# The lambda sums of an attention layer, from TensorE to VectorE

## The chip, the cores and the metric

The kernel runs on one core of a Trainium2 chip. The metric is the device time of one execution in microseconds (us), from launch to end. A core has TensorE (PE) for matrix products, with its weight loads shown as PEld, VectorE (DVE), ScalarE (ACT), GpSimd (POOL) and SyncE (SP), which here only issues transfers. The engines run their own lists of instructions and wait for each other through semaphores; 16 DMA engines move data between the chip's main memory (HBM) and the on-chip memory (SBUF).

## The reference

Two layers on x of 256 rows by 2048, both x + Mixer(RMSNorm(x)): a gated differential attention with 8 heads, then a gated Conformer convolution, and a last RMSNorm. Only the attention is touched, and in it the scalar lambda:

```python
h = xn @ w_in
q, k, v, gate = jnp.split(h, ...)
lam = (jnp.exp(jnp.sum(lq1 * lk1))
       - jnp.exp(jnp.sum(lq2 * lk2)) + lambda_init)
...
s = einsum(q, k) + bias
p = softmax(s)
a = p[:, :, 0] - lam * p[:, :, 1]
o = einsum(a, v)
```

lq1, lk1, lq2 and lk2 are vectors of 128 numbers. So lambda needs two products of 128 numbers, two sums and two exponentials, once for the layer.

## The kernel before, in words

Every product of the layers is made in three passes: activations and weights are both split in a high and a low part, and PE multiplies high by high, high by low and low by high. The weights come in chunks of 1 MB (four blocks of 128 rows, 512 columns, `w_raw`), into a ring of four. SP loads a chunk when the low part of the chunk four before it is done; ScalarE makes the high part (`high_part`, L473), VectorE the low part (`low_part`, L814), and then PE multiplies.

The attention's first product is worked through in four pairs of heads. A pair has 16 slots, one chunk each: slots 0 to 3 make q, 4 to 7 k, 8 to 11 v, 12 to 15 the gate. `pair_slot(j, i)` exists on PE, ScalarE and VectorE and puts the attention's own work between the chunks: the scaling of k at slots 7 and 8, the scores (PE: L1327 to L1329; VectorE: L898, L901, L902) and the softmax's exponentials (ScalarE: L548) at slots 9 and 10, lambda and the weighting of the two softmaxes at slot 11 (L907 to L917), the transposes (L932) and a's split (L573, L936) at slots 12 and 13, and A·V on PE at slot 14 (L1341 to L1343). Chunk numbers run on: slot i of pair 0 multiplies chunk i, while ScalarE and VectorE split chunk i + 4 there. Pair 0 is unrolled, and its first four chunks come in 16 small pieces (`HEAD`).

For lambda the four vectors are four columns behind the other per-feature vectors in one transfer (`vec_all`, L351). VectorE multiplies them pairwise behind head piece 8 (L852, 128x2). PE multiplies a 128x128 matrix of ones by these two columns behind slot 2 (`lambda_sums`, L1216), which sums over the partitions and leaves the sums on all of them. ScalarE takes the Exp from that bank (L510), behind the split of chunk 5 and ahead of the squares of x (L519). VectorE puts them together at slot 11 (L907).

What sets the order near it is written out by hand. SP's list in pair 0 is: chunk loads, the two halves of x behind chunks 5 and 6, the taps of the convolution (`dwT`, L370) behind chunk 7, and the bias windows (`bias_w`, L376) behind chunk 13. The windows are first made in HBM: GpSimd writes a line per head (L437), ScalarE stores the lines (L512) and expands them (`windows_dram`, L558), and SP waits for that (`windows_stored`) before it loads the bias. VectorE's first score step (L898) waits for the bias.

The bank for the lambda sums is also the one in which the norm's factor is spread over the partitions behind slot 6 (`spread_rstd`, L1204); the counts `a_full` and `a_free` give it to one and then the other.

## Time and profile before

| | |
|---|---|
| median of 3 runs | 826.24 us (825.64 to 827.05) |
| the profiled execution's own time | 825.33 us |
| its span, first to last instruction | 823.5 us |
| PE busy | 815.9 us (99%) |
| VectorE busy | 645.0 us (78%) |
| ScalarE busy | 449.3 us (55%) |
| GpSimd busy | 228.8 us (28%) |
| mean granted clock of PE | 0.998 |
| HBM traffic | 200 GB/s over the span |

A row of the timeline has the start, the duration and the engine, then the line of the kernel, the operation, output<-inputs, the shapes and the count; in brackets stands how long the engine sat idle before it and what ended that. A busy share is a mean over stages with different limits, so the stretch around the change has to be read by itself. Matmuls overlap in the pipeline: the distance from one start to the next is what one costs. All times in the rows are from the span's start.

### The profile page before, as it was taken

How to read it: one execution, taken by the hardware profiler on the slowest of the kernel's cores; microseconds unless marked ns; L12 is line 12 of the kernel's file. 1: busy time of each engine (PE TensorE's matmuls, PEld its weight loads, DVE VectorE, ACT ScalarE, POOL GpSimd, SP SyncE). 2: the span in 40 equal slices, each digit the busy share in tenths (PEclk: the TensorE clock that was granted, in tenths of full speed). 3: DMA queues.
4: the chain of work that ended last, by engine and by line, in shares of the span. 5: the costliest groups of instructions: out<-in, count | busy, mean ns of one | idle time of the engine just before them, and what ended most of it. 6: DMA issues, size and time to landing. Idle time of an engine off the chain costs nothing.

```text
span 823.5 us, 13844 instructions
## 1 busy us (share of the span) xinstructions
PE 815.9 (99%) x5628; PEld 754.6 (92%) x5628; DVE 645.0 (78%) x1095; ACT 449.3 (55%) x586; POOL 228.8 (28%) x107
## 2 busy tenths in 40 slices
PE   9999999999999999999999999999999999999996
PEld 9988899889998899888888999999999999998885
DVE  7579785797659785798788988999999998656651
ACT  7756643546436643555554465465555556594432
POOL 0300000000000000002000009988989987680000
PEclk9999999999999999999999999999999999999999
DMA  9987566536754566535655666655655565549502
GB/s 330 395 304 260 175 210 217 184 122 204 232 187 145 171 209 217 186 103 175 229 174 190 205 194 216 204 175 186 205 190 175 200 197 176 192 155 355 197 8 102
DMA packets 99809, 163.68 MB, mean 199 GB/s; under 512 B 3616, under 2 KB 40992, under 8 KB 99240
## 3 DMA queue, kind: packets, MB, share of 16 engines
q1 hardware_dynamic: 98128, 160.51, 58.0%
q10 hardware_dynamic: 1624, 2.38, 0.8%
q8 instruction: 39, 0.64, 0.3%
q14 instruction: 18, 0.15, 0.1%
HBM read 160.76 MB, written 3.69 MB: 200 GB/s over the span
## 4 chain that ended last, share of the span: by engine, by line
PE 94%; DMA 2%; DVE 1%; ACT 1%; SPq 1%; issue 0%; ACTq 0%
PE ps_acc L1242 16%; PE ps_acc L1244 16%; PE ps_acc L1245 16%; PE ps_acc L1228 14%; PE ps_acc L1230 14%; PE ps_acc L1231 14%; DMA sb_xs<-in_x 2%; DMA sb_w_raw<-in_attn_w_in 1%; PE ps_a L1204 0%; PE ps_d L1327 0%; PE ps_d L1329 0%; PE ps_a L1341 0%; PE ps_a L1343 0%; PE ps_d L1328 0%; PE ps_a L1342 0%
## 5 line engine op out<-in xcount | busy, mean ns | idle before, releaser
L473 ACT ACTIVATE sb_w_hi<-sb_w_raw 128x2048 fp32r<-128x2048 f32 x139 | 265.7, 1919 | 224.0 <-PE ps_acc L1245 151.3
L445 POOL TENSOR_TENSOR sb_w_lo<-sb_w_raw,sb_w_hi 128x2048 fp32r<-128x2048 f32 x45 | 208.2, 4634 | 387.3 <-ACT sb_w_hi L473 387.3
L814 DVE TENSOR_TENSOR sb_w_lo<-sb_w_raw,sb_w_hi 128x2048 fp32r<-128x2048 f32 x94 | 213.6, 2289 | 91.7 <-ACT sb_w_hi L473 91.3
L1242 PE MATMUL ps_acc<-sb_conv_hi,sb_w_hi 128*128 128x256 f32 x768 | 213.0, 277 | 0.0
L1245 PE MATMUL ps_acc<-sb_conv_hi,sb_w_lo 128*128 128x256 f32 x768 | 212.1, 276 | 0.0
L1244 PE MATMUL ps_acc<-sb_conv_lo,sb_w_hi 128*128 128x256 f32 x768 | 212.1, 276 | 0.0
L1045 DVE SCALAR_TENSOR_TENSOR ps_d<-sb_uT,sb_dwT,ps_d 128x256 f32<-128x256 f32 x480 | 189.3, 517 | 4.5 <-ACT ps_d L704 4.5
L1228 PE MATMUL ps_acc<-sb_w_hi,sb_act_hi 128*128 128x512 f32 x384 | 149.7, 390 | 0.0
L1230 PE MATMUL ps_acc<-sb_w_lo,sb_act_hi 128*128 128x512 f32 x384 | 149.6, 390 | 0.0
L1231 PE MATMUL ps_acc<-sb_w_hi,sb_act_lo 128*128 128x512 f32 x384 | 149.4, 389 | 0.0
L1244 PEld LDWEIGHTS ps_acc<-sb_conv_lo,sb_w_hi 128*128 128x128 f32 x768 | 144.2, 188 | 0.0
L1242 PEld LDWEIGHTS ps_acc<-sb_conv_hi,sb_w_hi 128*128 128x128 f32 x768 | 144.2, 188 | 0.0
L1245 PEld LDWEIGHTS ps_acc<-sb_conv_hi,sb_w_lo 128*128 128x128 f32 x768 | 144.2, 188 | 0.0
L1242 PE MATMUL ps_acc<-sb_act_hi,sb_w_hi 128*128 128x256 f32 x448 | 123.8, 276 | 0.2 <-DVE sb_w_lo L814 0.2
L1245 PE MATMUL ps_acc<-sb_act_hi,sb_w_lo 128*128 128x256 f32 x448 | 123.7, 276 | 0.0
L1244 PE MATMUL ps_acc<-sb_act_lo,sb_w_hi 128*128 128x256 f32 x448 | 123.7, 276 | 0.0
L1231 PEld LDWEIGHTS ps_acc<-sb_w_hi,sb_act_lo 128*128 128x128 f32 x384 | 72.1, 188 | 15.1
L1228 PEld LDWEIGHTS ps_acc<-sb_w_hi,sb_act_hi 128*128 128x128 f32 x384 | 72.1, 188 | 14.9 <-DVE sb_act_lo L983 0.4
L1230 PEld LDWEIGHTS ps_acc<-sb_w_lo,sb_act_hi 128*128 128x128 f32 x384 | 72.1, 188 | 14.4
L1242 PEld LDWEIGHTS ps_acc<-sb_act_hi,sb_w_hi 128*128 128x128 f32 x448 | 84.1, 188 | 0.6 <-DVE sb_w_lo L814 0.5
L1244 PEld LDWEIGHTS ps_acc<-sb_act_lo,sb_w_hi 128*128 128x128 f32 x448 | 84.1, 188 | 0.1
L1245 PEld LDWEIGHTS ps_acc<-sb_act_hi,sb_w_lo 128*128 128x128 f32 x448 | 84.1, 188 | 0.0
(166 smaller groups left out, 875.3 us busy)
## 6 DMA issues: line engine op xcount, KB each, us to landing
sb_w_raw<-in_attn_w_in SPq DMA_DIRECT2D x59, 1024.0 KB, 5.8
sb_w_raw<-in_conv_w_in SPq DMA_DIRECT2D x64, 512.0 KB, 4.6
sb_w_raw<-in_attn_w_out SPq DMA_DIRECT2D x16, 1024.0 KB, 5.0
sb_w_raw<-in_conv_w_in SPq DMA_DIRECT2D x16, 1024.0 KB, 5.1
sb_w_raw<-in_conv_w_out SPq DMA_DIRECT2D x16, 1024.0 KB, 5.0
sb_w_raw<-in_attn_w_in SPq DMA_DIRECT2D x15, 256.0 KB, 4.6
sb_xs<-in_x SPq DMA_DIRECT2D x2, 1024.0 KB, 13.4
sb_x_in<-in_x_turned SPq DMA_DIRECT2D x15, 128.0 KB, 4.3
```

The lines of the kernel that those rows point to most:

```text
L445: pool.tensor_tensor(w_part(w_lo, c), w_raw[c % RING][:], w_part(w_hi, c).bitcast(F32), ALU.subtract).then_inc(lo_ready_pool, 1)
L473: act.activation(w_part(w_hi, c if like is None else like), w_raw[slot][:], ACT.Copy).then_inc(hi_ready, 1)
L814: dve.tensor_tensor(w_part(w_lo, like), w_raw[slot][:], w_part(w_hi, like).bitcast(F32), ALU.subtract).then_inc(lo_ready, 1)
L1045: dve.scalar_tensor_tensor(out_, uT[:, k, tap:tap + SEQ], dwT[:, k, tap:tap + 1], out_, ALU.mult, ALU.add).then_inc(tap_done, 1)
L1228: pe.matmul(into, left_hi, high[:, k], start=(kt == 0 and not filled), stop=False, skip_group_check=filled)
L1230: pe.matmul(into, left_hi, low[:, k], start=False, stop=False, skip_group_check=filled)
L1231: ins = pe.matmul(into, left_lo, high[:, k], start=False, stop=(kt == KT - 1), skip_group_check=filled)
L1242: pe.matmul(into, left_hi, hi[:, kt], start=(kt == 0 and f % 2 == 0), stop=False, skip_group_check=True)
L1244: pe.matmul(into, left_hi, lo[:, kt], start=False, stop=False, skip_group_check=True)
L1245: ins = pe.matmul(into, left_lo, hi[:, kt], start=False, stop=(kt == KT - 1), skip_group_check=True)
```

## The change

The four lambda vectors are an input of their own, laid end to end (512 numbers). SP reads them with one transfer whose source repeats for each of the 128 partitions, behind the load of chunk 8, into a part of `mT` that is not yet in use. At slot 9 of pair 0, ahead of the first score step, VectorE multiplies them pairwise along the free axis (128x256) and sums each half (128x2). ScalarE takes the Exp behind the softmax's exponentials of slot 10. The product with ones on PE, its wait and its bank hand-over go, as does the small product on VectorE. Semaphores are renamed and recounted with it.

```diff
-VECS_AT, LAM_AT = 4, 8
+VECS_AT = 4
...
-        lam_in = vec_all[:, 8 * KT:8 * KT + 4]
...
-        lam_prod = small[:, 4:6]
+        lam_sum = small[:, 4:6]
         lam_exp = small[:, 6:8]
         neg_lam = small[:, 8:9]
...
                 rstd_bc = mT[:, KT - 1]
+                lam_in = mT[:, KT - 3:KT - 1].rearrange("p a (b n) -> p (a b) n", b=2)
+                lam_prod = mT[:, KT - 4].rearrange("p (a n) -> p a n", a=2)
...
-        lam_prod_ready, lam_exp_ready = sem("lam_prod_ready"), sem("lam_exp_ready")
+        lam_landed, lam_prod_ready, lam_sum_ready = sem("lam_landed"), sem("lam_prod_ready"), sem("lam_sum_ready")
+        lam_exp_ready, neg_lam_ready, head_scaled = sem("lam_exp_ready"), sem("neg_lam_ready"), sem("head_scaled")
...
-        A_START, A_PER_PAIR = 2, 2
+        A_START, A_PER_PAIR = 1, 2
...
                 if p == VECS_AT:
-                    sp.dma_start(vec_all[:, 0:8 * KT + 4], vectors).then_inc(vecs_landed, 16)
+                    sp.dma_start(vec_all[:, 0:8 * KT], vectors).then_inc(vecs_landed, 16)
             sp.dma_start(table[:], rel_bias).then_inc(table_landed, 16)
...
                         if first and t == 1 and i == NCH - 1:
                             sp.dma_start(dwT[:], taps).then_inc(taps_landed, 16)
+                        if first and t == 2 and i == 0:
+                            sp.dma_start(lam_in, bass.AP(lambdas.tensor, lambdas.offset, [[0, P], [1, 4 * HD]])
+                                         ).then_inc(lam_landed, 16)
                         if (t, i) == ((3, 1) if first else (0, NCH - 1)):
                             if first:
                                 sp.wait_ge(windows_stored, 16)
...
-            act.wait_ge(a_full, 1)
-            act.activation(lam_exp, bank_a[0][:, 0:2], ACT.Exp).then_inc(a_free, 1)
             act.wait_ge(line_ready, len(bucket_runs()) + 1)
             act.dma_start(line_dram, line[:]).then_inc(line_stored, 16)
 
             act.activation(vecs[:, G_HEAD, :], vecs[:, G_HEAD, :], ACT.Copy, scale=1.0 - LAMBDA_INIT
-                           ).then_inc(lam_exp_ready, 1)
+                           ).then_inc(head_scaled, 1)
...
                                            ).then_inc(exp_done, 1)
+                    if type(j) is int and (j, i) == (0, 10):
+                        act.wait_ge(lam_sum_ready, 1)
+                        act.activation(lam_exp, lam_sum, ACT.Exp).then_inc(lam_exp_ready, 1)
                     return
...
                 if i == 7:
-                    act.wait_ge(a_full, 2)
+                    act.wait_ge(a_full, 1)
                     act.activation(rstd_bc, bank_a[0][:, 0:SEQ], ACT.Copy).then_inc(a_free, 1)
-                    act.wait_ge(a_free, 2 + 2)
+                    act.wait_ge(a_free, 2 + 1)
                 pair_slot(0, i)
...
-                if p == LAM_AT:
-                    dve.wait_ge(vecs_landed, 16)
-                    dve.tensor_tensor(lam_prod, lam_in[:, 0:4:2], lam_in[:, 1:4:2], ALU.mult
-                                      ).then_inc(lam_prod_ready, 1)
...
                     if type(j) is int and j == 0:
-                        dve.wait_ge(a_free, 2 + 2)
+                        dve.wait_ge(a_free, 2 + 1)
                     dve.wait_ge(w_free, RING + NCH * (4 * j + 2))
...
+                if i == 9 and type(j) is int and j == 0:
+                    dve.wait_ge(lam_landed, 16)
+                    dve.tensor_tensor(lam_prod, lam_in[:, 0:4:2], lam_in[:, 1:4:2], ALU.mult).then_inc(lam_prod_ready, 1)
+                    dve.wait_ge(lam_prod_ready, 1)
+                    dve.tensor_reduce(lam_sum, lam_prod, AX.X, ALU.add).then_inc(lam_sum_ready, 1)
                 if i == 8:
...
                 if i == 11:
                     if type(j) is int and j == 0:
-                        dve.wait_ge(a_free, 2 + 1)
+                        dve.wait_ge(lam_exp_ready, 1)
                         dve.scalar_tensor_tensor(neg_lam, lam_exp[:, 1:2], -LAMBDA_INIT, lam_exp[:, 0:1],
-                                                 ALU.add, ALU.subtract).then_inc(lam_prod_ready, 1)
-                        dve.wait_ge(lam_prod_ready, 2)
+                                                 ALU.add, ALU.subtract).then_inc(neg_lam_ready, 1)
+                        dve.wait_ge(neg_lam_ready, 1)
 
                     dve.wait_ge(exp_done, 8 * (j + 1))
                     link(dve.reciprocal(row_inv, row_sum))
...
-            def free_a(n):
-                pe.wait_ge(a_free, n + 1)
...
-            def lambda_sums():
-
-                free_a(0)
-                pe.wait_ge(lam_prod_ready, 1)
-                pe.matmul(bank_a[0][:, 0:2], ones[:], lam_prod, start=True, stop=True).then_inc(a_full, 1)
...
             for i in range(16):
                 pair_slot(0, i)
-                if i == 2:
-                    lambda_sums()
                 if i == 6:
-                    spread_rstd(1, 1)
+                    spread_rstd(0, 1)
...
-                               ("attn_head_gain", "conv_dw_b", "conv_ln_g", "conv_ln_b", "conv_b_in",
-                                "attn_lq1", "attn_lk1", "attn_lq2", "attn_lk2")])
+                               ("attn_head_gain", "conv_dw_b", "conv_ln_g", "conv_ln_b", "conv_b_in")])
+    lambdas = np.concatenate([inputs[name].reshape(-1) for name in ("attn_lq1", "attn_lk1", "attn_lq2", "attn_lk2")])
...
         "vectors": features.T,
+        "lambdas": lambdas,
```

VectorE, around slot 9 of pair 0, before: w_lo0 is the low part of chunk 12, ps_d0 and ps_d1 are the banks of the scores.

```order
L814 TENSOR_TENSOR sb_w_lo0<-sb_w_raw0,sb_w_hi0 128x2048 [waits hi_ready]
L898 SCALAR_TENSOR_TENSOR sb_probs<-ps_d0,sb_small,sb_bias_w 128x512 [waits d_full,a_full,bias_landed]
L901 TENSOR_REDUCE sb_small<-sb_probs 128x2 [waits d_free]
L902 TENSOR_SCALAR sb_small<-sb_small 128x2 [waits dve_done]
L898 SCALAR_TENSOR_TENSOR sb_probs<-ps_d1,sb_small,sb_bias_w 128x512 [waits d_full]
L901 TENSOR_REDUCE sb_small<-sb_probs 128x2 [waits d_free]
```

And with the change, from the same low part on:

```order
L820 TENSOR_TENSOR sb_w_lo0<-sb_w_raw0,sb_w_hi0 128x2048 [waits hi_ready]
L887 TENSOR_TENSOR sb_mT<-sb_mT 128x256 [waits lam_landed]
L889 TENSOR_REDUCE sb_small<-sb_mT 128x2 [waits lam_prod_ready]
L905 SCALAR_TENSOR_TENSOR sb_probs<-ps_d0,sb_small,sb_bias_w 128x512 [waits d_full,a_full,bias_landed]
L908 TENSOR_REDUCE sb_small<-sb_probs 128x2 [waits d_free]
L909 TENSOR_SCALAR sb_small<-sb_small 128x2 [waits dve_done]
L905 SCALAR_TENSOR_TENSOR sb_probs<-ps_d1,sb_small,sb_bias_w 128x512 [waits d_full]
L908 TENSOR_REDUCE sb_small<-sb_probs 128x2 [waits d_free]
```

Two operations stand between chunk 12's low part and the first score step; `mT` holds the vectors and the products. The first has a wait for the new transfer.

SP in pair 0, from chunk 5's load on, before (in_x is x by rows, in_taps the taps, window_scratch the bias windows):

```order
L342 DMA sb_w_raw<-in_attn_w_in 128x4x512 [waits lo_ready]
L368 DMA sb_xs<-in_x 128x2048
L342 DMA sb_w_raw<-in_attn_w_in 128x4x512 [waits lo_ready]
L368 DMA sb_xs<-in_x 128x2048
L342 DMA sb_w_raw<-in_attn_w_in 128x4x512 [waits lo_ready]
L370 DMA sb_dwT<-in_taps 128x496
L342 DMA sb_w_raw<-in_attn_w_in 128x4x512 [waits lo_ready] x6
L376 DMA sb_bias_w<-window_scratch 128x2x384 [waits windows_stored]
```

And with the change:

```order
L344 DMA sb_w_raw<-in_attn_w_in 128x4x512 [waits lo_ready]
L370 DMA sb_xs<-in_x 128x2048
L344 DMA sb_w_raw<-in_attn_w_in 128x4x512 [waits lo_ready]
L370 DMA sb_xs<-in_x 128x2048
L344 DMA sb_w_raw<-in_attn_w_in 128x4x512 [waits lo_ready]
L372 DMA sb_dwT<-in_taps 128x496
L344 DMA sb_w_raw<-in_attn_w_in 128x4x512 [waits lo_ready]
L374 DMA sb_mT<-in_lambdas 128x512
L344 DMA sb_w_raw<-in_attn_w_in 128x4x512 [waits lo_ready] x5
L381 DMA sb_bias_w<-window_scratch 128x2x384 [waits windows_stored]
```

One transfer has come between chunk 8's load and the five that follow it, ahead of the bias; it waits for nothing of its own.

ScalarE between chunk 5's split and chunk 6's, before (ps_a is the bank of the lambda sums):

```order
L473 ACTIVATE sb_w_hi<-sb_w_raw 128x2048 [waits w_free,chunk_landed1]
L510 ACTIVATE sb_small<-ps_a 128x2 [waits a_full]
L512 DMA line_scratch<-sb_line 8x512 [waits line_ready]
L514 ACTIVATE sb_vec_all<-sb_vec_all 128x16
L519 ACTIVATE sb_probs,sb_small<-sb_xs 128x2048 [waits rows_landed0]
L473 ACTIVATE sb_w_hi<-sb_w_raw 128x2048 [waits w_free,chunk_landed2,ss_ready]
```

And with the change:

```order
L478 ACTIVATE sb_w_hi<-sb_w_raw 128x2048 [waits w_free,chunk_landed1]
L515 DMA line_scratch<-sb_line 8x512 [waits line_ready]
L517 ACTIVATE sb_vec_all<-sb_vec_all 128x16
L522 ACTIVATE sb_probs,sb_small<-sb_xs 128x2048 [waits rows_landed0]
L478 ACTIVATE sb_w_hi<-sb_w_raw 128x2048 [waits w_free,chunk_landed2,ss_ready]
```

The Exp at the second row and its wait for PE are gone; it now stands behind the last Exp of slot 10.

## Rows read from the trace of the kernel before

**Rows 1.** The page's part 1: busy time, share of the span, instructions

```profile
PE 815.9 (99%) x5628; PEld 754.6 (92%) x5628; DVE 645.0 (78%) x1095; ACT 449.3 (55%) x586; POOL 228.8 (28%) x107
```

**Rows 2.** Waits of PE: waiter <- releaser: us in total, times, longest

```profile
PE ps_d L1348 <- POOL sb_ones L423: 1.0, 1, 1.0
PE ps_acc L1242 <- DVE sb_w_lo L814: 0.2, 1, 0.2
```

**Rows 3.** Timeline of PE, 21 to 91 us: start, duration, instruction

```profile
21.37 0.28 PE L1216 MATMUL ps_a<-sb_small,sb_ones 128*128 128x2 f32 x2
21.51 0.70 PE L1291 MATMUL ps_acc<-sb_act_hi,sb_w_hi 128*128 128x256 f32 x4
...
43.99 0.39 PE L1242 MATMUL ps_acc<-sb_act_hi,sb_w_hi 128*128 128x256 f32 x1 [0.25 <-DVE sb_w_lo L814]
...
90.46 0.28 PE L1341 MATMUL ps_a<-sb_v_hi,sb_q_hi 128*128 128x256 f32 x1
```

**Rows 4.** The chain that ended last, 17 to 45 us: start, us

```profile
19.39 15.62 DMA sb_xs<-in_x
...
41.64 2.30 DVE sb_w_lo L814
```

**Rows 5.** Timeline of VectorE, 14 to 90 us

```profile
14.65 0.15 DVE L852 TENSOR_TENSOR sb_small<-sb_vec_all 128x2 f32<-128x2 f32 x1
...
59.30 2.29 DVE L814 TENSOR_TENSOR sb_w_lo<-sb_w_raw,sb_w_hi 128x2048 fp32r<-128x2048 f32 x1 [1.04 <-ACT sb_w_hi L473]
62.49 0.75 DVE L898 SCALAR_TENSOR_TENSOR sb_probs<-ps_d,sb_small,sb_bias_w 128x512 f32<-128x512 f32 x1 [0.90 <-DMA sb_bias_w<-window_scratch]
63.28 0.69 DVE L901 TENSOR_REDUCE sb_small<-sb_probs 128x2 f32<-128x512 f32 x1
...
68.20 0.75 DVE L898 SCALAR_TENSOR_TENSOR sb_probs<-ps_d,sb_small,sb_bias_w 128x512 f32<-128x512 f32 x1 [0.26 <-PE ps_d L1329]
...
71.36 2.28 DVE L814 TENSOR_TENSOR sb_w_lo<-sb_w_raw,sb_w_hi 128x2048 fp32r<-128x2048 f32 x1
...
75.43 0.48 DVE L917 SCALAR_TENSOR_TENSOR sb_probs<-sb_probs,sb_small 128x256 f32<-128x256 f32 x1
75.83 0.35 DVE L915 TENSOR_SCALAR sb_probs<-sb_probs,sb_small 128x256 f32<-128x256 f32 x1
...
88.79 1.29 DVE L936 TENSOR_TENSOR sb_q_lo<-sb_probs,sb_q_hi 128x512 fp32r<-128x512 f32 x2 [0.70 <-ACT sb_q_hi L573]
```

**Rows 6.** Timeline of ScalarE, 28 to 76 us

```profile
28.84 0.14 ACT L510 ACTIVATE sb_small<-ps_a 128x2 f32<-128x2 f32 x1
...
35.03 1.93 ACT L519 ACTIVATE sb_probs<-sb_xs 128x2048 f32<-128x2048 f32 x1 [0.56 <-DMA sb_xs<-in_x]
...
74.34 1.27 ACT L568 ACTIVATE sb_v_hi<-ps_acc,sb_small 128x512 fp32r<-128x512 f32 x2 [1.76 <-PE ps_acc L1231]
```

**Rows 7.** Timeline of SP's queue, 23 to 60 us: start of issue, us

```profile
23.42 3.16 SPq L370 DMA_DIRECT2D sb_dwT<-in_taps  x1
26.65 0.40 SPq L342 DMA_DIRECT2D sb_w_raw<-in_attn_w_in  x1
...
31.29 1.26 SPq L342 DMA_DIRECT2D sb_w_raw<-in_attn_w_in  x1
...
59.55 0.37 SPq L376 DMA_DIRECT2D sb_bias_w<-window_scratch  x1
```

**Rows 8.** DMA issues: count, KB each, median us from issue to landing

```profile
sb_w_raw<-in_attn_w_in SPq DMA_DIRECT2D x59, 1024.0 KB, 5.8
...
sb_b_out_bc<-in_conv_b_out SPq DMA_DIRECT2D x1, 1024.0 KB, 7.1
...
sb_vec_all<-in_vectors SPq DMA_DIRECT2D x1, 66.0 KB, 4.3
```

**Rows 9.** Windows: length, busy PE, PEld, DVE, ACT, POOL, PEclk, DMA share, GB/s

```profile
46.00:54.00 8.00, 8.00 (x53) 7.24 (x52) 5.78 (x5) 3.39 (x3) 0.00 (x0) 1.00 1.03 372
54.00:64.00 10.00, 10.00 (x52) 8.50 (x51) 7.23 (x7) 6.90 (x6) 0.00 (x0) 1.00 0.61 209
```

More of the change, by code:

```diff
@@ L72, in bucket_runs, with build @@
     return [(at, upto, int(bucket[at])) for at, upto in zip(starts, starts[1:] + [rel.size])]
-def build(nc, x, x_turned, vectors, taps, final_gain, rel_bias, attn_w_in, attn_w_out, conv_w_in,
+def build(nc, x, x_turned, vectors, lambdas, taps, final_gain, rel_bias, attn_w_in, attn_w_out, conv_w_in,
           conv_w_out, conv_b_out, out):
```

## The prediction

> **What bounds the kernel now.** I read the totals first, then TensorE's waits, then its rows in order of time, then the engines that hand it work in pair 0, and last the DMAs. TensorE (PE) is busy for 815.9 of 823.5 us [rows 1]. Its whole list of waits has two lines, 1.0 us before the first matmul and 0.2 us once for a low part of the weights [rows 2]; the second is the 0.25 us ahead of the matmul at 43.99 us [rows 3]. So an edit moves the end in only three ways: it takes matmuls off the stream, it changes one of these two waits, or it makes a new one. The rest of the 7.6 us that PE isn't busy lies after its last matmul, where nothing is edited.
>
> The wait at 43.99 is the start of chunk 7. The chain that ended last runs through it: the transfer of the second half of x ends at 35.01, ScalarE squares it at 35.03, then come the root, the q copies and chunk 7's split on ScalarE, and VectorE's low part at 41.64, done at 43.94 [rows 4, 6]. What releases PE there is a transfer in the full DMA queue, and no lambda step.
>
> **The matmul that goes.** The matmul of 128x2 starts at 21.37 and the next one starts at 21.51 [rows 3]: 0.14 us of PE. It pays nothing as long as the next stop stands: PE comes to chunk 7 at 43.6 instead of 43.74 and waits 0.39 us instead of 0.25. Value taken: 0. If the cover were gone (chunk 7 ready in time) it would be a gain of 0.14, with the wait 0.39. That is the lower bound of the whole change.
>
> **What goes from the other engines.** VectorE loses a product of 128x2 (0.15 us at 14.65, [rows 5]) and ScalarE an Exp (0.14 us at 28.84, [rows 6]). Both lie ahead of 35.03, where ScalarE idles for the x transfer anyway (0.56 us, [rows 6]); 0. The Exp moves behind the eight of pair 0's second score slot, which use the same function, so I count no table load, and 0.14 us there. ScalarE then stands idle for 1.76 us until the next v copy [rows 6], which covers it. The vectors' transfer of 66 KB [rows 8] loses 2 KB, 3% of it; 0.
>
> **The transfer that is added.** 128 rows of 2 KB, 256 KB, go on SP's queue between chunk 8's load (issued 26.65) and chunk 9's (31.29) [rows 7]. SP has 4.2 us there, since chunk 9's load waits for a low part. The slowest issue in sight, that of the taps, took 3.16 us [rows 7], so even that would not delay chunk 9's issue. The data do delay what follows: the DMA share is 1.03 from 46 to 54 us at 372 GB/s [rows 9]. At that rate 262144 B are 0.70 us of all engines. Nearest row for the price: weights have the same rows of 2 KB and make up this stretch. Other end: the one broadcast in the trace (b_out, also 128 rows, 8 KB each) took 7.1 us to land [rows 8], 1.8 us for a quarter of the bytes, or all 7.1 if rows and not bytes set it. I take 0.70 and keep both ends; call it d.
>
> The Trainium skill's page "DMA: Bandwidth & Descriptors", section "Anatomy of one DMA — SWDGE (gpsimd) path", gives a transfer some 2.0 us of fixed cost beside its bytes at 436 GB/s; it speaks of transfers that GpSimd issues. By it the estimate for this one is 2.6 us; were all of that time taken from the queue, d would be 2.6. The 16 engines' share near 1.0 at 372 GB/s says that one transfer's fixed part lies beside the next one's data, so I don't add it; what it would do is part of the second rival.
>
> Which loads are late by d: chunks 9 to 13, the window store (ScalarE's queue, same DMA engines) and behind it the bias load, which SP issues at 59.55 when the store is done [rows 7]. From 54 to 64 us the share is only 0.61 [rows 9], so the store could also make up some of d. The weights have room: chunk 12's low part ends at 61.59 [rows 5], and PE takes chunk 12 only when chunk 11 is done, at 74.3 by the v copy that waits for it [rows 6].
>
> **The two VectorE operations that are added.** Product 128x256: between 0.35 (one tensor with a scalar, 128x256) and 0.48 (two tensors, 128x256) [rows 5], 0.42. Reduction of 128x256 to 128x2: one of 128x512 is 0.69 [rows 5], so between 0.35 and 0.69, 0.43 with a fixed part. Two hand-overs of 0.04: 0.93 us, bounds 0.75 to 1.25. They stand behind chunk 12's low part and ahead of the first score step. There VectorE idles 0.90 us, from 61.59 to 62.49, for the bias load [rows 5]. Without d the sum is then 61.59 + 0.93 + 0.04 = 62.56, 0.07 late. With d both sides move: chunk 12 lands 0.7 later, and so does the bias: the score step starts at about 63.26, 0.77 late.
>
> **What is late next.** Behind the score step on VectorE stand all of pair 0's softmax, the 16 transposes and a's low part, and PE waits for the last at its A·V step. On the way one idle gives some back: 0.26 us at 68.20, where VectorE waits for PE's scores, which are not later [rows 5]. Nothing else does: the 0.70 us at 88.79 waits for ScalarE, which waits for the transposes. a's low part ends at 90.08 (88.79 + 1.29, [rows 5]); PE starts A·V at 90.46 without a wait [rows 3]. With the 0.05 us of a hand-over (43.94 to 43.99, [rows 3, 4]) the room is 0.33. So the new wait is 0.77 - 0.26 - 0.33 = 0.18 us, and in general d - 0.52, if that is above 0. The next lambda step (the 128x1 operation ahead of the reciprocal) was there before. It now waits for the Exp, which comes 0.2 us after the last softmax Exp (done at 72.58, the 74.34 of the v copy less its 1.76 of idle time, [rows 6]), at some 72.8 before any delay; VectorE is busy with chunk 14's low part until 73.64 [rows 5], so 0.
>
> Behind pair 0 VectorE idles for more than a microsecond at a time, and the later pairs are as before. A wait of PE is never given back, since PE is busy to the end.
>
> **Sum.** Against the profiled execution of 825.33 us (span 823.5, 1.8 us around it): 0 for the matmul + 0.18 for the wait = 825.5. That execution lies 0.9 us under the median of the runs, 826.24; on the median the forecast is 826.4.
>
> **Rivals.**
> First, all hidden: the window store makes up d in its half-empty stretch, the bias lands at 62.5 as before, and only 0.07 us of lateness is left, less than the 0.26. For it: share 0.61 from 54 to 64 [rows 9]. Against: the store's own end is what SP waits for, so something paces it. Time 826.2.
>
> Second, slower: the broadcast holds the queues much longer than its bytes. Mechanism: all 128 rows read the same 2 KB, as b_out's read one row. Everything turns on A·V at 90.46: from d = 0.52 on PE waits d - 0.52, and from d = 2.2 on that is over 0.2%. With 1.8 us the wait is 1.3 and the time 827.5; with 7.1 it is 6.6 and 832.8. For it: 7.1 us to landing against 5.8 for as many bytes of weights [rows 8]. Against: b_out's landing holds time queued behind weights too. By the page named above (2.6 us) the wait would be 2.1 and the time 828.3; the trace so far speaks for a fixed part that lies beside other data.
>
> Third, faster: in the full queue of the head the x transfer ends earlier. The smaller vectors rows are the only thing in front of it, at most 66 KB at 372 GB/s, 0.18 us; with the matmul's 0.14 that is 0.32, and 0.39 if the wait goes wholly. Time 825.9. Against: just 2 KB leave, and any time that PE gains at 43.99 is lost in part at 90.46, since the bias does not come earlier.
>
> **How the numbers follow.** No change means within 0.2%, 1.65 us, about what a measurement of this kernel can tell. Forecast (a small wait at A·V, 0 to 0.5 us) 0.62; all hidden 0.20; slower 0.10, of which 0.08 is beyond 1.65 us; faster 0.08, of which 0.03 is left for more than the 0.39 that I can find. So 0.03 faster, 0.89 same, 0.08 slower. The runs of before lie from 0.6 under to 0.8 over their median. The range takes the third rival with that spread (825.9 - 0.6) and the second with its 1.8 us and some of it: 825.3 to 827.8.
>
> **What would show it.** Right: PE's row at the start of chunk 7 with a wait of about 0.4 us instead of 0.25, at the same time near 44.0; two new VectorE rows of 0.4 us each between chunk 12's low part and the first score step; the score step near 63.3; a wait of 0 to 0.5 us ahead of A·V at 90.5; the bias issue 0 to 0.7 us later than 59.55. Wrong: a wait at A·V over 1 us (d mis-sized), chunk 7 starting well ahead of 44 (the head's queue moved), or any new wait of PE behind pair 0.

## The result and the profile after

The changed kernel takes 827.49 us (median of 20 runs, 826.41 to 829.2), the kernel before 826.21 us (20 runs beside them, 825.32 to 829.07). The ratio is 1.0014 with an interval of 1.0008 to 1.0020: inside 0.2%, and yet measurably slower, by some 1.3 us. The forecast of 826.4 us was 1.1 us too low; the time lies inside the stated range of 825.3 to 827.8. The profiled execution took 827.74 us (span 826.0), against 825.33 us (span 823.5). These two executions lie 2.41 us apart and the medians 1.28, so the sizes read from the rows are those of one pair of executions.

The page's totals after, to be held against [rows 1]:

```profile
PE 816.1 (99%) x5626; PEld 754.5 (91%) x5626; DVE 645.6 (78%) x1096; ACT 449.1 (54%) x586; POOL 229.6 (28%) x107
```

PE's busy time is the same to 0.2 us, so the difference is waiting. Its whole list of waits (waiter, releaser: us in total, times, longest) has three lines where [rows 2] had two:

```profile
PE ps_a L1339 <- issue: 1.6, 1, 1.6
PE ps_d L1346 <- POOL sb_ones L428: 1.0, 1, 1.0
PE ps_acc L1240 <- DVE sb_w_lo L820: 0.9, 1, 0.9
```

The first is new, and it is pair 0's A·V step. The last is the start of chunk 7. The rows of both on PE's timeline (start, duration, instruction, idle time before it):

```profile
44.59 0.38 PE L1240 MATMUL ps_acc<-sb_act_hi,sb_w_hi 128*128 128x256 f32 x1 [0.87 <-DVE sb_w_lo L820]
...
92.81 0.36 PE L1339 MATMUL ps_a<-sb_v_hi,sb_q_hi 128*128 128x256 f32 x1 [1.58 <-issue]
```

A·V starts 2.35 us after the 90.46 of [rows 3]. Of that, 1.58 is the new wait and 0.77 PE brought along; 0.60 of the 0.77 is the later chunk 7. The list puts the wait down to "issue", so it names no releaser. VectorE's timeline shows what A·V waited for: a's low part, the last row here, is done at 92.70, 0.11 us before A·V starts (before: [rows 5]):

```profile
60.49 2.29 DVE L820 TENSOR_TENSOR sb_w_lo<-sb_w_raw,sb_w_hi 128x2048 fp32r<-128x2048 f32 x1 [0.97 <-ACT sb_w_hi L478]
...
62.70 0.42 DVE L887 TENSOR_TENSOR sb_mT<-sb_mT 128x256 f32<-128x256 f32 x1
63.15 0.42 DVE L889 TENSOR_REDUCE sb_small<-sb_mT 128x2 f32<-128x256 f32 x1
...
65.46 0.75 DVE L905 SCALAR_TENSOR_TENSOR sb_probs<-ps_d,sb_small,sb_bias_w 128x512 f32<-128x512 f32 x1 [1.89 <-DMA sb_bias_w<-window_scratch]
...
70.82 0.74 DVE L905 SCALAR_TENSOR_TENSOR sb_probs<-ps_d,sb_small,sb_bias_w 128x512 f32<-128x512 f32 x1
...
91.41 1.29 DVE L943 TENSOR_TENSOR sb_q_lo<-sb_probs,sb_q_hi 128x512 fp32r<-128x512 f32 x2 [0.70 <-ACT sb_q_hi L579]
```

The two added operations take 0.42 us each and hold up nothing: behind them VectorE still waits 1.89 us for the bias. The first score step comes 2.97 us later than before, at 65.46. The idle 0.26 us that [rows 5] show at 68.20 is gone from the second step (70.82), so it was given back; the rest, up to a's low part, runs as before to within 0.1 us. So the sum is 2.97 - 0.26 (given back) - 0.33 (room at A·V) - 0.77 (PE later itself) = 1.61, and the row says 1.58. The bias is late because it is issued late. SP's queue after (start of issue, time for which SP is held, transfer; before: [rows 7]):

```profile
23.75 3.70 SPq L372 DMA_DIRECT2D sb_dwT<-in_taps  x1
27.50 0.58 SPq L344 DMA_DIRECT2D sb_w_raw<-in_attn_w_in  x1
28.12 4.98 SPq L374 DMA_DIRECT2D sb_mT<-in_lambdas  x1
33.15 0.57 SPq L344 DMA_DIRECT2D sb_w_raw<-in_attn_w_in  x1
37.38 0.37 SPq L344 DMA_DIRECT2D sb_w_raw<-in_attn_w_in  x1
44.56 0.37 SPq L344 DMA_DIRECT2D sb_w_raw<-in_attn_w_in  x1
...
62.44 0.37 SPq L381 DMA_DIRECT2D sb_bias_w<-window_scratch  x1
```

The added transfer holds SP for 4.98 us, chunk 9's load goes out at 33.15 instead of 31.29, and the bias at 62.44 instead of 59.55. The rows at 37.38 and 44.56 are the loads of chunks 10 and 11. ScalarE's rows show where the window store is issued and the load that comes late most visibly, chunk 10's (L478), first after the change, then before it:

```profile
39.22 0.80 ACTq L564 DMA_DIRECT2D window_scratch<-line_scratch  x1
...
49.25 1.93 ACT L478 ACTIVATE sb_w_hi<-sb_w_raw 128x2048 fp32r<-128x2048 f32 x1 [2.34 <-DMA sb_w_raw<-in_attn_w_in]
```

```profile
38.63 0.80 ACTq L558 DMA_DIRECT2D window_scratch<-line_scratch  x1
...
46.33 1.93 ACT L473 ACTIVATE sb_w_hi<-sb_w_raw 128x2048 fp32r<-128x2048 f32 x1 [0.57 <-DMA sb_w_raw<-in_attn_w_in]
```

So the store lasts, from its issue to the bias issue that waits for it, 20.9 us before and 23.2 us after. It starts 0.6 us later and runs 2.3 us longer: that is the whole lateness of the bias. The question for the experiments is what makes the store longer.

### The profile page after: what moved, and what is told of

It is laid out like the page before. It is cut to its first block, busy times and chain, and to the rows that moved or that the text cites. A ratio compares the mean times of both kernels' runs of the same rounds, so it can differ in the third digit from the quotient of the medians.

```text
span 826.0 us, 13841 instructions
## 1 busy us (share of the span) xinstructions
PE 816.1 (99%) x5626; PEld 754.5 (91%) x5626; DVE 645.6 (78%) x1096; ACT 449.1 (54%) x586; POOL 229.6 (28%) x107
## 4 chain that ended last, share of the span: by engine, by line
PE 94%; DMA 2%; DVE 1%; ACT 1%; SPq 1%; issue 1%; ACTq 0%
PE ps_acc L1240 16%; PE ps_acc L1243 16%; PE ps_acc L1242 16%; PE ps_acc L1226 14%; PE ps_acc L1228 14%; PE ps_acc L1229 14%; DMA sb_xs<-in_x 2%; DMA sb_w_raw<-in_attn_w_in 1%; PE ps_a L1339 0%; PE ps_a L1211 0%; PE ps_d L1327 0%; PE ps_d L1325 0%; PE ps_a L1341 0%; PE ps_d L1326 0%; PE ps_a L1340 0%
## 5 line engine op out<-in xcount | busy, mean ns | idle before, releaser
L478 ACT ACTIVATE sb_w_hi<-sb_w_raw 128x2048 fp32r<-128x2048 f32 x139 | 265.5, 1918 | 224.5 <-PE ps_acc L1243 151.4
```

Source lines behind the costliest of these rows:

```text
L478: act.activation(w_part(w_hi, c if like is None else like), w_raw[slot][:], ACT.Copy).then_inc(hi_ready, 1)
```

## Experiments

The theories. **Bytes:** the 256 KB take DMA time from the store, more than the 0.70 us that I priced, because of when they come. **One row:** 128 reads of the same 2 KB are slow. **Held SP:** not the data but the 4.98 us for which SP can't issue chunk 9's load pushes the loads into the store. **Compute:** the moved operations, not the transfer. All eleven kernels were timed against the kernel before on the same chip. In each diff "-" is the changed kernel's code, unless it says otherwise. A table of all stands behind them.

**The changed kernel again.**

> The changed kernel once more. It separates what belongs to the change from what was chance in its one profile. If the late start of chunk 7 there (44.59 instead of 43.99 us) was chance of the head's transfers, chunk 7 starts at 43.9 to 44.2 here; if it belongs to the change, at 44.5 to 44.7. In both cases the wait of PE ahead of A.V should be there, 0.5 to 2 us, and the time 1.0 to 1.6 us over the kernel before.

827.48 us against 826.19, ratio 1.0014 (1.0004 to 1.0023). The profiled execution took 830.66 us. The list of waits:

```profile
PE ps_a L1339 <- issue: 2.1, 1, 2.1
...
PE ps_acc L1240 <- DVE sb_w_lo L820: 1.0, 1, 1.0
```

SP's queue:

```profile
30.28 3.40 SPq L374 DMA_DIRECT2D sb_mT<-in_lambdas  x1
...
63.64 0.37 SPq L381 DMA_DIRECT2D sb_bias_w<-window_scratch  x1
```

The same wait at the same place, and a store of 23.7 us (issued at 39.91).

**The kernel before again.**

> The kernel before once more, for a second profile of it. The profiles of the changed kernel and of the two experiments without or with the transfer alone have chunk 7 on PE at 44.6 to 45.4 us, the run with 128 different rows at 43.7. If that is chance of the head's transfers, this profile may also lie anywhere from 43.7 to 45.4; if it belongs to the change, it is again at 43.9 to 44.1. Either way no wait ahead of A.V, bias issue 20 to 22 us after the window store's issue, and a ratio of 1 within 0.1%.

826.48 against 826.49, 0.9996 (0.9987 to 1.0005). PE comes to A·V without a wait, as before:

```profile
90.96 0.28 PE L1341 MATMUL ps_a<-sb_v_hi,sb_q_hi 128*128 128x256 f32 x1
```

Chunk 7 starts at 44.46 here and at 43.99 in [rows 3]: the same kernel scatters by half a microsecond in the head. (The expectation above has 43.7 for the run with 128 different rows; its trace has 44.19.)

**Everything but the transfer.** GpSimd fills the room with a constant instead of lambda.

```diff
-                        if first and t == 2 and i == 0:
-                            sp.dma_start(lam_in, bass.AP(lambdas.tensor, lambdas.offset, [[0, P], [1, 4 * HD]])
-                                         ).then_inc(lam_landed, 16)
+            pool.wait_ge(lo_ready, RING + 1)
+            pool.memset(lam_in, 0.03).then_inc(lam_landed, 16)
```

> Leaves the transfer of the lambda vectors out: GpSimd fills their place with a constant in the time in which it has nothing to do, so lambda has another value. All the VectorE and ScalarE work of the change stays. Theory T (the added transfer makes the window store end late, and through the bias A.V): bias issue back at 59 to 60 us, no wait at A.V, 826.2 +- 0.4. Rival O (the two added VectorE operations take the room ahead of A.V): wait and time as in the changed kernel, 827.3 to 827.7. My recorded sum would give 826.2 here too.

826.69 against 826.19, 1.0004 (0.9995 to 1.0012): not told from no change. The store is back to 20.5 us. SP's queue:

```profile
59.97 0.37 SPq L378 DMA_DIRECT2D sb_bias_w<-window_scratch  x1
```

PE's row at A·V:

```profile
91.29 0.28 PE L1338 MATMUL ps_a<-sb_v_hi,sb_q_hi 128*128 128x256 f32 x1
```

No wait at A·V. It comes 0.83 us later than in [rows 3] because chunk 7 started at 44.82, without any added transfer.

**The transfer alone**, in the kernel before ("+" against that one); its data go unused, and VectorE only waits for them at the lambda step.

```diff
+                        if first and t == 2 and i == 0:
+                            sp.dma_start(lam_wide, bass.AP(lambdas.tensor, lambdas.offset, [[0, P], [1, 4 * HD]])
+                                         ).then_inc(lam_landed, 16)
...
+                        dve.wait_ge(lam_landed, 16)
```

> The kernel before, with only the new transfer at its place in SP's list, landing in the same unused memory; VectorE waits for it at slot 11, long after it is there. Theory T: bias issue 61.5 to 62.5 instead of 59.55, a wait at A.V of 0.5 to 2 us, 827.0 to 827.7. Rival O: no wait, 826.2 +- 0.3.

827.44 against 826.19, 1.0015 (1.0005 to 1.0024): the whole loss, with none of the moved operations. SP's queue:

```profile
28.16 5.80 SPq L374 DMA_DIRECT2D sb_mT<-in_lambdas  x1
...
62.39 0.37 SPq L381 DMA_DIRECT2D sb_bias_w<-window_scratch  x1
```

PE's row at A·V:

```profile
92.92 0.36 PE L1347 MATMUL ps_a<-sb_v_hi,sb_q_hi 128*128 128x256 f32 x1 [0.83 <-issue]
```

With the run without the transfer this rules out the compute theory. The wait at A·V is shorter (0.83), as PE itself is 1.63 us late there: chunk 7 started at 45.41.

**128 different rows** in place of one row read 128 times.

```diff
-                            sp.dma_start(lam_in, bass.AP(lambdas.tensor, lambdas.offset, [[0, P], [1, 4 * HD]])
-                                         ).then_inc(lam_landed, 16)
+                            sp.dma_start(lam_in, lambdas.rearrange("p (a n) -> p a n", n=HD)).then_inc(lam_landed, 16)
...
-        "lambdas": lambdas,
+        "lambdas": np.broadcast_to(lambdas, (P, 4 * HD)),
```

> The changed kernel, but its input holds the 512 numbers 128 times and the transfer reads 128 different rows of 2 KB. Rival R (128 reads of one row are slow): the issue no longer blocks SP for 5 us, the bias issue is back near 60, time 826.3 +- 0.4. Theory T: nothing changes, 827.2 to 827.8, SP blocked for 4 to 5 us.

827.11 against 826.19, 1.0011 (1.0001 to 1.0021). SP's queue:

```profile
27.35 5.08 SPq L374 DMA_DIRECT2D sb_mT<-in_lambdas  x1
...
61.81 0.37 SPq L380 DMA_DIRECT2D sb_bias_w<-window_scratch  x1
```

PE's row at A·V:

```profile
92.23 0.36 PE L1338 MATMUL ps_a<-sb_v_hi,sb_q_hi 128*128 128x256 f32 x1 [1.38 <-issue]
```

SP is held as long (5.08 us), the store lasts 23.3 us as in the changed kernel (23.2) and the wait is there. The one-row theory falls.

**The transfer on ScalarE's queue**, so that SP isn't held.

```diff
-                            sp.dma_start(lam_in, bass.AP(lambdas.tensor, lambdas.offset, [[0, P], [1, 4 * HD]])
-                                         ).then_inc(lam_landed, 16)
+            act.wait_ge(lo_ready, RING + 1)
+            act.dma_start(lam_in, bass.AP(lambdas.tensor, lambdas.offset, [[0, P], [1, 4 * HD]])).then_inc(lam_landed, 16)
```

> The changed kernel with the transfer issued from ScalarE's queue behind the store of the lines, at about 29 us, in place of SP's. Same bytes, same time, but SP is not held up. Theory I (SP is blocked for 5 us by the issue, so the loads of chunks 9 and 10 come later and fall into the time in which the window store would run fast): chunk 9 issued at 31 to 32 us, bias issue 20 to 21 us after the store's, no wait at A.V, 826.2 to 826.7. Rival B (the bytes alone do it): bias issue 22 to 24 us after the store's, wait of 0.8 to 2 us, 827.1 to 827.6.

827.22 against 826.49, 1.0007 (0.9998 to 1.0016). ScalarE's queue:

```profile
29.54 0.36 ACTq L514 DMA_DIRECT2D sb_mT<-in_lambdas  x1
```

SP's queue:

```profile
31.73 1.55 SPq L344 DMA_DIRECT2D sb_w_raw<-in_attn_w_in  x1
...
61.91 0.37 SPq L378 DMA_DIRECT2D sb_bias_w<-window_scratch  x1
```

PE's row at A·V:

```profile
92.26 0.36 PE L1338 MATMUL ps_a<-sb_v_hi,sb_q_hi 128*128 128x256 f32 x1 [1.06 <-issue]
```

The issue costs 0.36 us, chunk 9's load goes out near its old time (31.73), and still the store lasts 22.7 us and A·V waits 1.06. So the held SP is at most a part of it. How large a part stays open: the time lies between the two kernels, and its interval holds both.

**The transfer 21 us later**, behind chunk 13's load and ahead of SP's wait for the store.

```diff
-                        if first and t == 2 and i == 0:
-                            sp.dma_start(lam_in, bass.AP(lambdas.tensor, lambdas.offset, [[0, P], [1, 4 * HD]])
-                                         ).then_inc(lam_landed, 16)
...
                             if first:
+                                sp.dma_start(lam_in, bass.AP(lambdas.tensor, lambdas.offset, [[0, P], [1, 4 * HD]])
+                                             ).then_inc(lam_landed, 16)
                                 sp.wait_ge(windows_stored, 16)
```

> The changed kernel with the transfer issued by SP behind the load of chunk 13, just ahead of the wait for the window store, where the DMA engines are half idle. Theories I and B alike: bias issue 20 to 21.5 us after the store's; the vectors land at 58 to 61.5, so VectorE waits little for them; wait at A.V 0 to 0.5, 826.2 to 826.8. Rival O (added VectorE work): 827.3 or more.

826.12 against 826.49, 0.9997 (0.9987 to 1.0007). SP's queue:

```profile
49.38 0.68 SPq L375 DMA_DIRECT2D sb_mT<-in_lambdas  x1
...
59.19 0.37 SPq L380 DMA_DIRECT2D sb_bias_w<-window_scratch  x1
```

VectorE's first score step:

```profile
63.60 0.75 DVE L904 SCALAR_TENSOR_TENSOR sb_probs<-ps_d,sb_small,sb_bias_w 128x512 f32<-128x512 f32 x1 [0.43 <-DMA sb_bias_w<-window_scratch]
```

PE's row at A·V:

```profile
91.07 0.28 PE L1338 MATMUL ps_a<-sb_v_hi,sb_q_hi 128*128 128x256 f32 x1
```

The same bytes, beside the same store, cost nothing here: 19.95 us of store and no wait at A·V. The time of the kernel before is back; the interval lies clear of the changed kernel's 1.0008 to 1.0020, though it touches that of the second measurement, 1.0004 to 1.0023. It isn't the bytes as such, but when they come.

**The transfer behind the bias load, the product on GpSimd, the sums on ScalarE.**

```diff
+            pool.wait_ge(lam_landed, 16)
+            pool.tensor_tensor(lam_prod, lam_in[:, 0:4:2], lam_in[:, 1:4:2], ALU.mult).then_inc(lam_prod_ready, 1)
...
+                        for a in range(2):
+                            act.activation(lam_in[:, a], lam_prod[:, a], ACT.Copy, accum_out=lam_sum[:, a:a + 1]
+                                           ).then_inc(lam_sum_ready, 1)
...
-                    dve.tensor_tensor(lam_prod, lam_in[:, 0:4:2], lam_in[:, 1:4:2], ALU.mult).then_inc(lam_prod_ready, 1)
-                    dve.tensor_reduce(lam_sum, lam_prod, AX.X, ALU.add).then_inc(lam_sum_ready, 1)
```

> The transfer behind the bias load, GpSimd makes the product, ScalarE the sums (two copies of 128x128 with a running sum behind slot 9's exponentials, in idle time). Neither the window store nor VectorE's path to A.V has anything added. Theories I and B: no wait at A.V, 826.0 to 826.5, the kernel before within noise. If 827 or more, the loss has another source than the store and the path (the missing matmul, the order of ScalarE, the instructions' places).

826.16 against 826.49, 0.9998 (0.9989 to 1.0007). GpSimd's product:

```profile
67.10 2.54 POOL L454 TENSOR_TENSOR sb_mT<-sb_mT 128x256 f32<-128x256 f32 x1 [37.94 <-DMA sb_mT<-in_lambdas]
```

The split of chunk 14 on ScalarE, then its low part on VectorE:

```profile
70.97 1.92 ACT L480 ACTIVATE sb_w_hi<-sb_w_raw 128x2048 fp32r<-128x2048 f32 x1 [0.60 <-DMA sb_w_raw<-in_attn_w_in]
...
72.92 2.29 DVE L827 TENSOR_TENSOR sb_w_lo<-sb_w_raw,sb_w_hi 128x2048 fp32r<-128x2048 f32 x1 [0.71 <-ACT sb_w_hi L480]
```

PE's row at A·V:

```profile
91.75 0.36 PE L1341 MATMUL ps_a<-sb_v_hi,sb_q_hi 128*128 128x256 f32 x1 [0.77 <-issue]
```

Time as before, yet with a wait of 0.77 at A·V in its profile, where none was expected. VectorE waits 0.71 us for the split of chunk 14. ScalarE's added sums are done before that split, which waits 0.60 us for its load; and that load now stands behind the bias and the added transfer in SP's list. Taking work off VectorE gained nothing, as VectorE's 0.84 us were free.

**The transfer twice.**

```diff
+                            sp.dma_start(lam_spare, bass.AP(lambdas.tensor, lambdas.offset, [[0, P], [1, 4 * HD]])
+                                         ).then_inc(lam_landed, 16)
...
-                    dve.wait_ge(lam_landed, 16)
+                    dve.wait_ge(lam_landed, 32)
```

> The changed kernel with the transfer made twice, one behind the other, into two places (512 KB). Theory B (its bytes push the loads of chunks 9 and 10 into the time in which the window store would run fast): the store takes longer again, 24 to 26 us from its issue to the bias issue (20.5 to 20.9 before, 23.2 changed), wait at A.V 2.5 to 4 us, 828 to 830. Rival F (the store has lost its fast stretch already, more bytes cost only their own time, 0.7 us): 23.5 to 24.2 us, wait about 2.2, 827.8 to 828.5. If the store's end had nothing to do with the bytes: as the changed kernel, 827.5.

827.75 against 826.18, 1.0023 (1.0013 to 1.0033): 0.3 us over the changed kernel, which the intervals don't tell apart. PE's wait:

```profile
PE ps_a L1342 <- issue: 1.9, 1, 1.9
```

SP's queue:

```profile
27.21 5.10 SPq L375 DMA_DIRECT2D sb_mT<-in_lambdas  x1
32.35 0.57 SPq L377 DMA_DIRECT2D sb_mT<-in_lambdas  x1
...
61.85 0.37 SPq L384 DMA_DIRECT2D sb_bias_w<-window_scratch  x1
```

The second 256 KB add little: the store lasts 23.5 us, not 25 or more. It looks as if the first transfer had already taken something that can be lost only once.

**The store issued earlier**, behind chunk 6's split.

```diff
+                    act.wait_ge(line_stored, 16)
+                    act.dma_start(windows_dram, bass.AP(line_dram.tensor, line_dram.offset + P - 1,
+                                                       [[REL, HEADS], [-1, P], [1, BW]])).then_inc(windows_stored, 16)
...
-                if i == 4 and type(j) is int and j == 0:
-                    act.wait_ge(line_stored, 16)
-                    act.dma_start(windows_dram, bass.AP(line_dram.tensor, line_dram.offset + P - 1,
-                                                       [[REL, HEADS], [-1, P], [1, BW]])).then_inc(windows_stored, 16)
```

> The changed kernel with the transfer where it is, but ScalarE issues the window store behind the split of chunk 6, at 34 to 35 us instead of 39.2. If the chain store -> bias -> score step -> A.V is what costs, the bias is issued some 2 to 4 us earlier than 62.4 and the wait at A.V is gone or under 0.4 us: 826.0 to 826.7, although the transfer is still there. Rival: the earlier store only takes room from x and chunk 7, PE waits longer there (1 us or more at 43.6) and the time stays at 827 or above.

827.69 against 826.18, 1.0016 (1.0005 to 1.0027): no cure, where 826.0 to 826.7 was expected. The bias goes out at 56.61 and A·V has no wait, which supports the chain, but PE waits at the scores instead, for a k part that comes behind chunk 10's late split. PE's wait:

```profile
PE ps_d L1323 <- DVE sb_k_lo L892: 1.6, 1, 1.6
```

ScalarE's split of chunk 10:

```profile
51.87 1.92 ACT L478 ACTIVATE sb_w_hi<-sb_w_raw 128x2048 fp32r<-128x2048 f32 x1 [2.66 <-DMA sb_w_raw<-in_attn_w_in]
```

**The late transfer, the early store, and chunk 7's split ahead of the second square.**

```diff
+                                sp.dma_start(lam_in, bass.AP(lambdas.tensor, lambdas.offset, [[0, P], [1, 4 * HD]])
+                                             ).then_inc(lam_landed, 16)
                                 sp.wait_ge(windows_stored, 16)
...
+                    act.wait_ge(line_stored, 16)
+                    act.dma_start(windows_dram, bass.AP(line_dram.tensor, line_dram.offset + P - 1,
+                                                       [[REL, HEADS], [-1, P], [1, BW]])).then_inc(windows_stored, 16)
+                    high_part(RING + 3, 3, 2)
...
-            high_part(RING + 3, 3, 2)
...
-                if i == 6:
+                if i == 7:
                     spread_rstd(0, 1)
```

> A version that could beat both: the transfer behind chunk 13's load, the window store early, and chunk 7's split on ScalarE and VectorE ahead of the second square of x and the root, with the spread of the norm's factor behind slot 7 instead of 6. Then neither A.V nor chunk 7 (0 to 1 us of wait in the profiles so far) has anything to wait for, and the 0.14 us of the missing matmul count: 825.2 to 825.9, 0.04 to 0.12% under the kernel before. Rival: chunk 7's load itself lands too late for it, PE waits as before, 826.0 to 826.5; or the factor comes too late for k, a new wait at slots 8 to 10, 826.5 or more.

826.21 against 826.18, 1.0002 (0.9993 to 1.0010). PE's list has one line left, that before the first matmul:

```profile
PE ps_d L1343 <- POOL sb_ones L427: 1.0, 1, 1.0
```

The wait at chunk 7 is gone, and the time isn't the 825.2 to 825.9 that was expected: it is that of the kernel before. A gain of 0.25 us for the wait would be too little to tell here. No kernel here beats the one before.

**What the runs say together.** "Store" is the time from the store's issue to the bias issue.

| kernel | transfer issued at | store, us | A·V starts (wait) | median - before |
|---|---|---|---|---|
| before | none | 20.9 | 90.46 (0) | 0 |
| before again | none | 20.5 | 90.96 (0) | 0.0 |
| no transfer | none | 20.5 | 91.29 (0) | +0.5 |
| behind chunk 13 | 49.38 | 19.95 | 91.07 (0) | -0.4 |
| behind the bias | 61.04 | 21.7 | 91.75 (0.77) | -0.3 |
| changed | 28.12 | 23.2 | 92.81 (1.58) | +1.3 |
| changed again | 30.28 | 23.7 | 94.06 (2.13) | +1.3 |
| transfer alone | 28.16 | 22.3 | 92.92 (0.83) | +1.25 |
| 128 rows | 27.35 | 23.3 | 92.23 (1.38) | +0.9 |
| ScalarE's queue | 29.54 | 22.7 | 92.26 (1.06) | +0.7 |
| twice | 27.21, 32.35 | 23.5 | 92.23 (1.9) | +1.6 |
| store early | 27.35 | 23.4 | no wait; 1.58 at the scores | +1.5 |
| late transfer, early store | 51.59 | 23.5 | 90.36 (0) | 0.0 |

With the transfer at its early place the store takes 22.3 to 23.7 us, without it there 19.95 to 21.7 (the two kernels with an early store are left out; they come below). Where the 2.3 us arise in the changed kernel shows in the packets. Counted in the trace, in steps of 2 us of the span: packets of the window store (1024 of 1536 B in all) and the packets of 2048 B of SP's queue:

```
from, us          40   42   44   46   48   50   52   54   56   58   60
before   store     0   55  180  222  110  116  114  114   98   15    0
         SP      374  320  130  179  275  268  311  187  124  161
after    store     0   27  108  172  119  112  119  109  116  108   34
         SP      381  347  239  195  269  276  297  232  124  119
later    store     0   25  221  260  109  114  116  113   60    6
 (x 13)  SP      379  349   98  106  272  280  298  306  167  195
twice    store     0   65  111  121  117  109  117  114  116  112   42
         SP      280  314  291  307  309  277  259  266  112  114
```

("Later" is the transfer behind chunk 13.) Beside loads the store runs at 55 to 60 packets per us. In these kernels it runs faster only from 44 to 48 us, at up to 130, and SP's queue runs low there: chunk 11's load is issued only when chunk 7's low part is done, at 43.96 before and 44.56 after. Before, 402 packets went in these 4 us, after, 280. The missing 122, at 57 per us, are 2.1 us, about the 2.3 us by which the store is longer. The late loads (chunk 10's above all) now fill the gap. With the transfer twice the gap is gone, which fits that more bytes cost little more. Behind chunk 13 the transfer is issued when the gap has passed, and the gap is intact.

The gap isn't the whole account, as three runs show. Cut the store at its 800th packet. In the kernel before, the first 800 take 11.1 us and the last 224 take 5.05; in the changed kernel 13.1 and 5.3, so there the loss lies in the front part, with the gap. But with the transfer alone it is 11.2 and 6.25, and on ScalarE's queue 11.3 and 6.6: the front part is as before, and the store is late in its last packets, for a reason that these runs don't show (the last 224 also scatter without an early transfer, from 5.05 to 6.1). And with the late transfer and the early store, SP's queue falls just as low from 48 to 50 us (104 packets), and the store doesn't run faster: it moves 104 packets there. In both kernels with an early store it has no fast stretch at all and takes 23.4 and 23.5 us, with the transfer early or late. So it is shown that, with the store issued where it was, the transfer at its early place makes it longer; that it does so by closing the gap is read off the changed kernel's trace, and no run shows it by itself.

The rate itself isn't explained. The Trainium skill's page "DMA: Bandwidth & Descriptors", section "Queues, rings and completion order", says that each DMA engine takes turns between the queues that have work for it. The trace of the kernel before agrees with it in the gap (up to 130 packets per us against 57 beside loads), but that of the kernel with the late transfer and the early store from 48 to 50 us doesn't, and neither does the end of the store after the change: from 56 to 60 us, SP's queue has fallen from 297 to 124 packets in 2 us, and the store stays at 116 and 108. The windows (length, busy PE, PEld, DVE, ACT, POOL, granted clock, DMA share, GB/s) say the same:

```profile
56.00:58.00 2.00, 2.00 (x11) 1.65 (x10) 1.98 (x1) 1.03 (x2) 0.00 (x0) 1.00 0.56 216
58.00:60.00 2.00, 2.00 (x11) 1.65 (x10) 1.52 (x3) 1.46 (x1) 0.00 (x0) 1.00 0.53 204
```

The engines stand half idle in the stretch in which the store ends late. So something else than their share paces it there; what, stays open.

## Why the prediction was nearly right, and where it failed

- **The place and the chain were right.** The only new wait of PE is at A·V, by way of the store, the bias and the first score step. The formula held: with the lateness that the profile shows it gives 1.61, the row 1.58. The 0.26 given back and the 0.33 of room were as read.
- **The step that failed is "I take 0.70 and keep both ends; call it d".** I counted the transfer's bytes at the full queue's rate. The store alone became 2.3 us longer (2.8 in the second profile of the changed kernel), and the bias issue 2.89 us later instead of 0 to 0.7. The prediction's own sign of a mis-sized d, a wait at A·V over 1 us, came. The row that I had gives the bytes' share of a full queue, but the store doesn't end by that: before the change more than a third of it went in 4 us in which SP's queue runs low, and in the changed kernel much of that stretch was lost. An average over 46 to 54 us [rows 9] hides it. Why the transfer alone and the one on ScalarE's queue lose their time later, in the store's last packets, stays open. Of the values that I kept, 0.70 and 1.8 lie under the 2.3 and only 7.1 over it. That the time is still inside the range is luck: the range reaches up to it only by the 1.8 of the second rival, whose mechanism the runs don't bear out.
- **"So even that would not delay chunk 9's issue" failed too.** I priced the issue by the taps' 3.16 us [rows 7] as the slowest in sight; it took 4.98, and the next load was 1.86 us late. As the run on ScalarE's queue shows, this is at most a part of the cause.
- **The first rival was wrong.** The store made up nothing in its half-empty stretch: after the change the engines' share is 0.56 and 0.53 from 56 to 60 us, and the store keeps its 54 to 58 packets per us.
- **The second rival had about the right time (827.5) by the wrong mechanism.** It put the price on reading one row 128 times; 128 different rows cost the same. The estimate that the prediction worked out from the Trainium skill's page "DMA: Bandwidth & Descriptors" (section "Anatomy of one DMA — SWDGE (gpsimd) path"), 2.6 us, comes near the measured 2.3, but the runs don't bear out a fixed cost taken from the queue: then the place 21 us later would have cost it too (19.95 us of store), and two transfers twice of it (23.5).
- **The added VectorE work was right:** 0.42 and 0.42 us against 0.42 and 0.43. I had let it make the score step 0.07 late without d; with the late transfer, where the store isn't longer, VectorE still waits 0.43 us for the bias behind it.
- **The matmul was worth nothing, as said.** It is gone, and the wait at chunk 7 took it up. But I expected chunk 7 "at the same time near 44.0" and it came at 44.59. The runs put it from 43.72 (the transfer twice) to 45.41 (the transfer alone), 44.82 without any transfer; that is scatter of the head, and I had no row for it from one profile. What causes it is open.
- **The wait for the Exp** was priced at 0, and PE has no wait behind A·V.

## What to carry to other kernels

Before pricing an added transfer by its bytes, look at what else shares the DMA engines, in steps of 2 us and queue by queue: a transfer that something waits for may have a short fast stretch, and an added transfer ahead of it can cost more than its own bytes (here 2.3 us of store against 0.70 by bytes). The same transfer, issued behind the last load that the head is short of, was free here, so the first thing to try with a small transfer that isn't needed soon is another place for it in the issue order. Read the scatter of a head from more than one profile before calling half a microsecond there an effect.

## What the runs showed of the hardware

- A DRAM-to-DRAM store in packets of 1536 B ran at 55 to 60 packets per us (57 x 1536 B = 88 GB/s) beside a stream of loads and also when the loads thinned out. At up to 130 (200 GB/s) it ran only between 44 and 50 us, while SP's queue ran low; in another stretch as low, 48 to 50 us of the kernel with the late transfer and the early store, it ran at 52.
- In the two thin stretches in which the store didn't speed up, both queues moved about equally many packets: 224 of the store and 243 of SP's from 56 to 60 us after the change, 104 and 104 from 48 to 50 us in the kernel with the late transfer and the early store.
- Issuing a 256 KB transfer behind chunk 8's load held SP for 3.40 to 5.80 us, a second one right behind it for 0.57; later ones held SP for 0.68 (at 49.38), 0.51 (at 51.59) and 0.76 (at 61.04), and the one on ScalarE's queue held ScalarE for 0.36.
- The product of 128x256 f32 took VectorE 0.42 us and GpSimd 2.54, six times as long, where the low parts of 128x2048 take them 2.29 and 4.6 us.
